# Modulation sums of a two-block model on one core: shared accumulators, fp32r row sums, and filler transposes at two seams

## The reference

```python
def reference(...):                      # 39 arrays, the first is x (1, 256, 2048)
    x = first_block(x, ...)              # attention + gated linear attention, then
                                         # x + (silu(h @ w_gate) * (h @ w_up)) @ w_down
    return second_block(x, c_2, ...)

def second_block(x, c, ...):
    c_act = jax.nn.silu(c)
    mod = (c_act @ w_ada[l] + b_ada[l])[:, None, :]        # w_ada is 2048 x 12288
    sh1, sc1, g1, sh2, sc2, g2 = jnp.split(mod, 6, axis=-1)
    h = rms_norm(x, norm_mix[l]) * (1.0 + sc1) + sh1
    x = x + g1 * hybrid_mixer(h, ...)
    h = rms_norm(x, norm_ffn[l]) * (1.0 + sc2) + sh2
    x = x + g2 * conv_glu_ffn(h, ...)                      # up, conv of width 3, silu gate, down
    return rms_norm(x, norm_final)
```

## Time and profile before

| | us |
|---|---|
| median of 3 runs | 2351.09 |
| range of the runs | 2350.31 to 2352.11 |
| profiled execution, its own time | 2352.51 |
| its span, first to last instruction | 2350.7 |
| PE busy | 2337.8 (99%) |
| DVE busy | 1616.4 (69%) |
| ACT busy | 1153.2 (49%) |
| mean granted TensorE clock | 0.997 of full |
| DMA, mean over the span | 543.62 MB, 231 GB/s |

### The profile page before, as it was taken

How to read it: one execution, slowest core, us unless ns; L and a number is a source line. 1 busy time by engine, 2 the same in 40 slices (tenths; PEclk the granted TensorE clock), 3 DMA queues, 4 the chain that set the end, 5 groups by cost and what they waited for, 6 DMA issues and landing times.

```text
span 2350.7 us, 43754 instructions
## 1 busy us (share of the span) xinstructions
PE 2337.8 (99%) x17937; PEld 2151.6 (92%) x17937; DVE 1616.4 (69%) x1931; ACT 1153.2 (49%) x1510; POOL 5.1 (0%) x7
## 2 busy tenths in 40 slices
PE   9999999999999999999999999999999999999998
PEld 8889778999999999888999899888999999998887
DVE  5668568777777766877778455667878666665556
ACT  5565454534344344444764444546544445454444
POOL 0000000000000000000000000000000000000000
PEclk9999999999999999999999999999999999999999
DMA  8556567888888877898577545555778656665563
GB/s 308 167 179 197 159 234 271 278 282 297 282 282 295 282 242 263 316 324 315 175 279 269 163 130 153 196 200 187 283 255 295 208 179 206 196 206 197 192 192 117
DMA packets 233049, 543.62 MB, mean 231 GB/s; under 512 B 15610, under 2 KB 22596, under 8 KB 232260
## 3 DMA queue, kind: packets, MB, share of 16 engines
q1 hardware_dynamic: 232756, 540.97, 68.3%
q10 hardware_dynamic: 144, 0.52, 0.1%
HBM read 535.11 MB, written 6.32 MB: 230 GB/s over the span
## 4 chain that ended last, share of the span: by engine, by line
PE 98%; DVE 0%; ACT 0%; issue 0%; DMA 0%; SPq 0%; DVEq 0%; ACTq 0%
PE ps L330 37%; PE ps L1858 18%; PE ps L608 18%; PE ps L2216 16%; PE ps L1875 2%; PE ps L2509 0%; PE ps L1041 0%; PE ps L1053 0%; PE ps L1071 0%; PE ps L1083 0%; PE ps L2141 0%; PE ps L460 0%; PE ps L2744 0%; PE ps L1134 0%; PE ps L2921 0%
## 5 line engine op out<-in xcount | busy, mean ns | idle before, releaser
L297 DVE TENSOR_TENSOR weights_lo<-raw_weights,weights_hi 128x1024 fp32r<-128x1024 f32 x786 | 957.6, 1224 | 659.8 <-ACT weights_hi L289 658.0
L289 ACT ACTIVATE weights_hi<-raw_weights 128x1024 fp32r<-128x1024 f32 x782 | 827.2, 1062 | 1086.8 <-PE ps L330 446.4
L516 DVE SCALAR_TENSOR_TENSOR ada_acc<-ada_w,col,ada_acc 128x1024 f32<-128x1024 f32 x180 | 230.2, 1279 | 0.1
L330 PE MATMUL ps<-conv_x_hi,weights_hi 128*128 128x256 f32 x1280 | 198.0, 277 | 0.0
L330 PE MATMUL ps<-glu_x_hi,weights_hi 128*128 128x256 f32 x1280 | 197.7, 276 | 0.0
L330 PE MATMUL ps<-glu_x_hi,weights_lo 128*128 128x256 f32 x1280 | 197.2, 276 | 0.0
L330 PE MATMUL ps<-glu_x_lo,weights_hi 128*128 128x256 f32 x1280 | 197.2, 276 | 0.0
L330 PE MATMUL ps<-conv_x_lo,weights_hi 128*128 128x256 f32 x1280 | 197.2, 276 | 0.0
L330 PE MATMUL ps<-conv_x_hi,weights_lo 128*128 128x256 f32 x1280 | 197.2, 276 | 0.0
L330 PEld LDWEIGHTS ps<-conv_x_hi,weights_hi 128*128 128x128 f32 x1280 | 169.1, 188 | 1.0 <-issue 1.0
L330 PEld LDWEIGHTS ps<-glu_x_hi,weights_hi 128*128 128x128 f32 x1280 | 169.0, 188 | 0.0
(11 more groups left out here) (560 smaller groups left out, 3635.3 us busy)
## 6 DMA issues: line engine op xcount, KB each, us to landing
raw_weights<-in_w_in_dram SPq DMA_DIRECT2D x202, 512.0 KB, 5.0
ada_w<-in_w_ada_dram SPq DMA_DIRECT2D x96, 1024.0 KB, 6.1
raw_weights<-in_w_ffn_up_dram SPq DMA_DIRECT2D x176, 512.0 KB, 4.6
raw_weights<-in_w_gate_dram SPq DMA_DIRECT2D x88, 512.0 KB, 4.6
raw_weights<-in_w_up_dram SPq DMA_DIRECT2D x88, 512.0 KB, 4.6
raw_weights<-in_w_down_dram SPq DMA_DIRECT2D x88, 512.0 KB, 5.7
raw_weights<-in_w_ffn_down_dram SPq DMA_DIRECT2D x88, 512.0 KB, 4.3
raw_weights<-in_w_out_dram SPq DMA_DIRECT2D x64, 512.0 KB, 5.1
```

Source lines behind the costliest of these rows:

```text
L289: kit.nc.scalar.activation(kit.slots(n, i)[0], raw, ACT.Copy).then_inc(kit.w_hi, 1)
L297: kit.nc.vector.tensor_tensor(lo, raw, hi.bitcast(F32), ALU.subtract).then_inc(kit.w_lo, 1)
L330: ins = nc.tensor.matmul(out, lhsT=lhsT, rhs=rhs, start=start and m == 0, stop=(k == KT - 1 and m == 2), skip_group_check=True)
L516: step = nc.vector.scalar_tensor_tensor(acc, w, c, acc, ALU.mult, ALU.add)
```

## The change

**Shared accumulators.** A step no longer takes 128 rows of one group. For groups 0 to 7 a step takes 16 rows of 8192 columns: row `r` and group `g` lie on partition `8 r + g`. One accumulator then holds all eight groups, each on every eighth partition, and 128 steps go over the 2048 rows, numbered as the steps of groups 0 to 7 were. For groups 8 and 9 a step takes 64 rows of 2048 columns, with 32 steps. Groups 10 and 11 stay as they were. The number of steps stays 192. Each step has its own DMA of 0.5 MB (192 DMAs). The accumulator is passed on: `Glu` ends with `ada_acc`, `Down` goes on from it into `ada_acc_oct` and then starts `ada_acc_half`, and the second mixer goes on from that into `ada_acc_9`.

**Columns of c.** The scalars for these steps are `c_2` repeated 8 times (`c_oct`, 128 columns) and twice (`c_half`, 32 columns). They are loaded as rows, widened by two DVE copies, and turned: the eighth pack is 128 wide instead of 96 and there is a ninth. In `Glu` a copy of 16 columns (`c_turn`) is made on DVE once a pass.

**Sums.** Nothing is summed in `Glu`. At seam 1 one set of eight matmuls against the mask `oct` (8 columns) gives all eight groups, at seam 2 one against `half` (2 columns) gives both. DVE adds the bias in `Ada.summed`. `last_scales` goes, and ACT's wait for it.

**Row sums.** Groups 10 and 11: ACT rounds the accumulator (`acc_hi`), DVE computes `acc_lo`, PE makes four fp32r matmuls of 512 columns for a group.

**Fillers.** At seam 1 `keep_busy` puts eight transposes before the turns, at seam 2 eleven in place of eight transposes of an accumulator and three fillers.

**The load of `final_w`** moves from ahead of `Down` to its load of unit pair 12, and waits there for `Down`'s first modulation step.

```diff
     def load(self, sp, lead, j, m):
...
-        w = kit.ins["w_ada_2"][0]
-        sp.dma_start(self.w[:, m % 2, :, :], w[2 * m * P:2 * (m + 1) * P, ds(2 * UN * lead + 2 * UN * j, 2 * UN)]
-                     .rearrange("(k p) n -> p k n", p=P)).then_inc(kit.ada_w[m % 2], 16)
+        for s in (2 * m, 2 * m + 1):
+            sp.dma_start(self.w[:, m % 2, s % 2, :], self.source(lead, j, s)).then_inc(kit.ada_w[m % 2], 16)
+    def source(self, lead, j, s):
+        w = self.kit.ins["w_ada_2"][0]
+        if lead < 8:
+            rows = w[ds(OCT * (16 * lead + s) + 16 * OCT * j, OCT), 0:16 * UN]
+        elif lead < 10:
+            rows = w[HALF * (16 * (lead - 8) + s):HALF * (16 * (lead - 8) + s + 1), 16 * UN:20 * UN]
+        else:
+            rows = w[P * s:P * (s + 1), 2 * UN * lead:2 * UN * (lead + 1)]
+        return rows.rearrange("r (g n) -> r g n", n=2 * UN)
...
+    def sums(self, pe, bank, mask, acc):
+        kit, (a, b) = self.kit, self.kit.at[mask]
+        n = b - a
         for q in range(8):
-            step = nc.tensor.matmul(kit.ps[:, bank, q:q + 1], lhsT=self.acc[:, q * P:(q + 1) * P],
-                                    rhs=kit.c("ones")[:, 0:1], start=True, stop=True)
+            step = kit.nc.tensor.matmul(kit.ps[:, bank, n * q:n * (q + 1)], lhsT=acc[:, q * P:(q + 1) * P],
+                                        rhs=kit.c(mask), start=True, stop=True)
         step.then_inc(kit.ada_sum, 1)
...  Glu, PE and DVE
-            mid = (lambda: self.ada.turned(pe, self.lead, j)) if summed else None
-                if summed and s == begun:
-                    self.ada.reduced(dve, self.lead, j)
-                    self.ada.product(dve, self.lead, j, 8 * half + s // 2)
+                    if q == 0:
+                        nc.vector.tensor_copy(self.c_turn[:, :], kit.col[:, ds(a + 16 * j, 16)]).then_inc(self.s_c, 1)
+                        dve.wait_ge(self.s_c, 1 + j)
+                    self.ada.product(dve, self.lead, j, q, c=self.c_turn[:, q:q + 1])
...  Down, SP
-        sp.wait_ge(kit.ada_sum, self.lead)
-        sp.dma_start(self.final_w[:, :], self.final_src).then_inc(kit.loaded, 16)
+                if k == 12:
+                    sp.wait_ge(kit.ada_acc, 16 * self.lead + 1)
+                    self.load_final(sp)
...  second mixer, PE
-        self.down.ada_sums(pe, 0)
-        self.down.ada_sums(pe, 1, 0, 2)
+        self.down.ada_sums(pe)
         pe.wait_ge(self.squares_in, 11)
         for k in range(4):
             self.turned.turn_early(pe, k)
-        self.down.ada_sums(pe, 1, 2, 8)
+        keep_busy(kit, 8, 7, S)
         for k in range(4):
             self.turned.turn(pe, k)
...  second mixer, DVE
+        self.down.ada_summed(dve)
         modulation(kit, 0)
         dve.wait_ge(self.s_root, 1)
...  ConvGlu
-        pe.wait_ge(kit.ada_acc, 16 * (self.lead + g + 1))
+        pe.wait_ge(self.s_acclo, g + 1)
         for b in range(2):
-            step = nc.tensor.matmul(kit.ps[:, 4 + 2 * g + b, :], lhsT=kit.c("ones"),
-                                    rhs=self.ada.acc[:, b * UN:(b + 1) * UN], start=True, stop=True)
+            for acc in (self.acc_hi, self.acc_lo):
+                step = nc.tensor.matmul(kit.ps[:, 4 + 2 * g + b, :], lhsT=self.ones[:, :], rhs=acc[:, b * UN:(b + 1) * UN],
+                                        start=acc is self.acc_hi, stop=acc is self.acc_lo)
         step.then_inc(kit.ada_sum, 1)
...
-                keep_busy(kit, 3, 7, S)
+                keep_busy(kit, 11, 7, S)
```

More of the change, by code:

```diff
@@ L503, in product, with scalar @@
+    def scalar(self, lead, s):
+        name, first = ("c_oct", 0) if lead < 8 else ("c_half", 8) if lead < 10 else ("c_2", lead)
+        return self.kit.cols(name, 16 * (lead - first) + s)
+    def product(self, dve, lead, j, s, acc=None, prior=None, c=None):
         nc, kit = self.kit.nc, self.kit
         m, k = s // 2, s % 2
[L505 to L509, removed]
@@ L827, in sync @@
         for n in range(1, len(self.packs)):
-            for at, to, width, src in self.packs[n][0]:
-                sp.dma_start(self.pack[at:to, n, 0:width], src).then_inc(self.s_packs, 16)
+            for at, to, lo, hi, src in self.packs[n][0]:
+                tile = {OCT: self.c_rows, HALF: self.c_rows_2}[hi] if hi in (OCT, HALF) else self.pack[:, n, :]
+                sp.dma_start(tile[at:to, lo:hi], src).then_inc(self.s_packs, 16)
         bias = self.mem["bias_dram"].ap()
@@ L944, in turn_pack @@
         _, w, _ = self.packs[n]
-        kit.nc.tensor.transpose(kit.ps[:, 6, 0:w], self.pack[0:w, n, :], kit.c("ident")[0:w, 0:w]
-                                ).then_inc(self.s_packT, 1)
+        last = n == len(self.packs) - 1
+        if n >= len(self.packs) - 2:
+            pe.wait_ge(self.s_cwide, 2)
+        rows = self.pack[0:w, 0 if last else n, :]
+        kit.nc.tensor.transpose(kit.ps[:, 6, 0:w], rows, kit.c("ident")[0:w, 0:w]).then_inc(self.s_packT, 1)
     def spread_scale(self, at):
@@ L1197, in scalar_side @@
             a = COLS["c_2"]
-            kit.act(nc.scalar.activation(kit.col[:, a:a + KT], kit.col[:, a:a + KT], ACT.Silu))
+            nc.scalar.activation(kit.col[:, a:a + KT], kit.col[:, a:a + KT], ACT.Silu).then_inc(self.s_csilu, 1)
+        if n == self.PACK + len(self.packs):
+            act.wait_ge(self.s_col, len(self.packs))
+            for a, b in ((COLS["c_half"], COLS["b_ada_2"]), (COLS["c_oct"], NCOLS)):
+                step = nc.scalar.activation(kit.col[:, a:b], kit.col[:, a:b], ACT.Silu)
+            step.then_inc(self.s_csilu, 1)
         for p in self.parts:
@@ L3574, in __init__ @@
             kit.sem("conv_" + n) for n in ("taps", "base", "sums", "silu", "glu"))
-        self.s_gate, self.s_scales = kit.sem("gate2_bias_in"), kit.sem("last_scales")
+        self.s_gate = kit.sem("gate2_bias_in")
+        self.acc_hi, self.acc_lo = (t(f"ada_acc_{n}", at, [P, 2 * UN], R32) for n, at in (("hi", 60), ("lo", 64)))
+        self.ones = t("ones_rounded", 92, [P, P], R32)
+        self.s_acchi, self.s_acclo = (kit.sem(n) for n in ("ones_and_ada_acc_hi", "ada_acc_lo"))
         self.down = None
@@ L3610, in scale_sums @@
     def scale_sums(self, pe):
-        kit, mixer = self.kit, self.mixer
-        pe.wait_ge(mixer.s_accs, 16)
-        pe.wait_ge(kit.pair_free[0], self.uses[0] + 1)
-        for q in range(8):
-            step = kit.nc.tensor.matmul(kit.ps[:, 1, q:q + 1], lhsT=mixer.accs[:, 0, q * P:(q + 1) * P],
-                                        rhs=kit.c("ones")[:, 0:1], start=True, stop=True)
-        step.then_inc(kit.ada_sum, 1)
-        pe.wait_ge(mixer.s_xlast, ST)
-        turn_sums(kit, mixer.accs[:, 1, :], 2).then_inc(kit.ada_sum, 1)
@@ L3722, in body @@
                         self.turned.scale_first(act, 3 + u // 2)
+                    g = self.acc_split(i, j, u, 1)
+                    if g is not None:
+                        act.wait_ge(kit.ada_acc, 16 * (self.lead + g + 1))
+                        if g == 0:
+                            nc.scalar.activation(self.ones[:, :], kit.c("ones"), ACT.Copy)
+                        else:
+                            act.wait_ge(kit.ada_sum, 2 + g)
+                        nc.scalar.activation(self.acc_hi[:, :], self.ada.acc, ACT.Copy).then_inc(self.s_acchi, 1)
                     if (j, u) == (1, 3):
```

229 lines of the change are left out of this document (100 added, 129 removed).

## The result

The changed kernel took 2421.0 us (median of 4 runs, 2394.4 to 2425.1) against 2351.6 before. The ratio of the means, with a fifth run of 2410.3 in it, is 1.0267, 95% interval 1.0203 to 1.0331. The forecast was 2342.0, faster by 0.4%. It is slower by 2.7%, and its runs lie 31 us apart where those before lay 2 apart. The profiled execution is the fastest of the four, 2394.39 us with a span of 2392.6; what its trace shows is thus 42 us of a loss whose median is 69; two longer executions of the same form of load are taken up further down.

The account below looks back on a forecast made before the run. PE was taken to bound the kernel (busy 2337.8 of 2350.7 us). Terms −5.5 − 1.7 − 2.2 (seam 1) + 0.1 + 0.2 = −9.1 us took the median 2351.09 to 2342.0, 8-in-10 range 2340.0 to 2345.8.

Parts of the forecast that it names:

- Loads: Modulation's 192 DMAs of 0.5 MB for 96 of 1 MB, and final_w among Down's loads: taken to cost 0.
- the loads come late (slower): Rival: the modulation's new load form slows the DMA queues and PE waits, +14 us in Down at 20%, 2356; chance 0.08.
- turned groups in `Glu`: Eight PE transposes for each of groups 0 to 5 go from the Glu passes: −5.5 us.
- row sums: Groups 10 and 11: four fp32r matmuls replace two fp32 ones and the slower products behind them: −1.7 us.
- seam 1, up to the turns: Less one-column work on PE lets the turns start at 1151.45 in place of 1152.32: −0.9 us.
- seam 1, clock: Clock stays full behind seam 1's turns: −1.46, with +0.2 for the next block, together −1.3 us.
- seam 2: DVE's bias step must end before the mean's last step, on the path; PE's queue keeps its length: +0.1 us.
- ninth pack: First mixer: PE turns one more pack, a unit taking 2.91 us against 2.72 without: +0.2 us.
- The DMA setup-cost knee: Skill's rule, about 2 us fixed cost a transfer: 192 us for 96 more DMAs without overlap; the prediction took 0.

Follow-up runs that it names:

- e5: Changed kernel, but loads of groups 0 to 7 take 4 KB from each of 128 rows, named as 16 outer rows of 8: median 2409.6 us.
- e8: Changed kernel, but loads of groups 0 to 7 take 4 KB from each of 128 rows, named as 32 outer rows of 4: median 2343.0 us.
- e9: Changed kernel with each modulation step's load, in all groups, cut into two DMAs of 0.25 MB to 64 partitions each: median 2372.8 us.
- e2: Changed kernel, but the 16 rows of each load of groups 0 to 7 lie 128 rows apart in memory: median 2410.2 us.
- e1: Changed kernel, but loads of groups 0 to 7 take 128 rows of 1024 columns again, one DMA of 0.5 MB a step: median 2343.6 us.
- e3: Changed kernel, but loads of groups 0 to 7 take 32 rows of 4096 columns, each on four partitions: median 2343.3 us.
- e4: Changed kernel, but loads of groups 0 to 7 take 64 rows of 2048 columns, each on two partitions: median 2343.2 us.
- e7: e3 without the eight filler transposes at seam 1: median 2344.5 us, ratio 0.9966 to the kernel before.

## Why the prediction was wrong

**The step that failed** is "Loads": "the bytes and the pieces of 4 KB are the same ... I take 0." The loads cost not 0 but 51 us in the profiled execution, and 67 in a longer one (e5). The pieces are the same; how the DMA names them is not. I had looked at the load as bytes and piece sizes, and the slow thing is the count of outer rows, which the diff shows (`OCT` rows) and no row of the trace before could have priced, since the loads of the modulation and of the weights all had 128 there. One argument of that step failed as well: SP's waits for a slot were read as a sign of room. In the changed kernel SP still waits as much, and PE waits too:

```profile
SPq L258 <- DVE weights_lo L302: 1408.5, 645, 7.4
```

The direction stood among the rivals, "the loads come late (slower)", with the right condition (a share of 1 in the queues), at 8 in 100 and 2356 us.

**How that rival was mis-sized.** Against e8, which differs from the changed kernel in the form of the loads alone, the profiled execution loses 51.4 us of span (2392.6 against 2341.2). The first product of `Down` starts at 939.76 against 902.73 and the sums of seam 1 at 1193.82 against 1142.23, the first rows of each pair being the changed kernel's:

```profile
939.76 0.73 PE L1862 MATMUL ps<-weights_hi,down_hi 128*128 128x512 f32 x2
...
1193.82 1.84 PE L514 MATMUL ps<-cst,ada_acc_oct 128*128 128x8 f32 x16
```

```profile
902.73 0.73 PE L1862 MATMUL ps<-weights_hi,down_hi 128*128 128x512 f32 x2
...
1142.23 1.84 PE L514 MATMUL ps<-cst,ada_acc_oct 128*128 128x8 f32 x16
```

Up to the first product of `Down` 37.0 us are lost, nearly all in `Glu`, and 14.6 in `Down`. Of the 51.4, 34.2 are time in which PE stands (48.2 against 14.0 us of the span) and 17.2 are longer busy time (2344.4 against 2327.2), of which the lower mean clock, 0.996 against 0.999, explains some 7 us as an estimate. For `Down` I had said 14, and that was luck: I took packets 20% longer, and from 960 to 1100 us they take 243 ns on average against e8's 181, 34% longer.

For `Glu` I had said that 17% of room protects it. From 520 to 860 us of e8, 7738 packets of 4 KB with a mean of 181 ns and 32264 of 2 KB with a mean of 98.8 fill 0.84 of the 16 engines' time. In the changed kernel the means are 268 and 106.5. As an estimate, e8's packets at these times would fill 1.01, so that the stream falls below what PE eats; DVE then waits for `ada_w`, `weights_lo` comes late, and PE stands. The measured share is 0.94, with fewer packets (7272 and 29631). At e9's means, 251 and 98.4 ns, the share is 0.96 and PE doesn't wait, and in the changed kernel itself PE is busy 99.85 of 100 us from 320 to 420 at a share of 1.01. So the share says where trouble is near, and not by itself that PE waits.

**The longer executions.** Other traces of the same form, near the median, show what the fast one doesn't. In e5 (2410.2 us) the first product of `Down` lies 36.0 us behind e8's (2 of them from before `Glu`) and the sums of seam 1 67.3, so `Down` lost 31 in place of 14.6, and PE's clock fell there:

```profile
960.00:1100.00 140.00, 122.78 (x496) 99.36 (x495) 85.00 (x87) 49.57 (x61) 0.10 (x1) 0.91 1.01 256
```

e2 (2411.1 us) shows the same, 34 and 68 us.

**The other terms** can be read in e8 and in the changed kernel, and were right:

| term | forecast | measured | where |
|---|---|---|---|
| turned groups in `Glu` | −5.5 | −5.6 | the hi products start 467.9 to 906.8 before and 467.3 to 901.5 in e8: −4.7 for five groups, and −0.6 at the start, in spite of the +0.3 of the ninth pack, for the first |
| row sums | −1.7 | −1.6 | 1775.24 to 1778.50 for sum and 20 products, 4.05 before |
| seam 1, up to the turns | −0.9 | −0.9 | 3.83 in e8 from sums to turns, 4.73 before |
| seam 1, clock | −1.3 | −1.3 | 4.23 and 3.48 for the two blocks, 5.80 and 3.18 before; the forecast's own numbers, −1.46 and +0.22, give −1.2 |
| seam 2 | +0.1 | +0.1 | 1655.32 to 1659.12 in the changed kernel, 3.66 before |
| ninth pack | +0.2 | +0.2 | 66.42 for the first L1026, 66.18 before |

Rows of the changed kernel at the row sum and at seam 2:

```profile
1775.24 0.40 PE L3616 MATMUL ps<-ada_acc_hi,ones_rounded 128*128 128x512 f32 x1
...
1776.17 0.64 PE L335 MATMUL ps<-conv_x_hi,weights_hi 128*128 128x256 f32 x4
...
1778.50 0.62 PE L335 MATMUL ps<-conv_x_hi,weights_lo 128*128 128x256 f32 x4
```

```profile
1655.32 0.60 PE L2145 MATMUL ps<-cst,conv_scaled 128*128 128x128 f32 x4
...
1659.12 0.68 PE L2134 MATMUL ps<-cst,conv_scaled 128*128 128x128 f32 x4 [0.27 <-DVE conv_scaled L2123]
```

The sum was −9.1; the span of e8 lies 9.5 below that of before and its median 8.7 below. The rule of the Trainium skill, "SBUF — State Buffer", The DMA setup-cost knee, weighed beside that step, had no part: with 96 DMAs more, e1, e3, e4 and e8 lie within 1.2 us of the forecast gain (8.0 to 8.7 us below the kernel before, against 9.1). What stays open is why the packets are slow, that is whether engines meet at a port, and why one execution of this form loses twice as much in `Down` as another.

## What to carry to other kernels

When a load changes its access pattern, compare the outermost dimension, not only bytes, piece size and partitions: 16 outer rows made the median packet of 4 KB 70% slower than 32, 64 or 128 outer rows, and loads to 64 partitions did the same with 64 outer rows. Price such a load in share of the DMA engines' time, for every stage that runs beside it, and take a share near 1 as a warning: here a stage at 0.82 was lost as surely as one at 0.88, and one at 0.96 (e9, `Glu`) was not. And a load that only an off-path product needs is on the path as soon as that product stands in an in-order list ahead of work that isn't.

## What I had not expected of the hardware

- The same 0.5 MB from the same DRAM addresses to the same 128 partitions lands in 7.9 us (median over the kernel) named as 16 x 8 pieces and in 5.3 named as 32 x 4 (e5, e8).
- The same DMA queues move 365 GB/s beside 64-row loads and 265 to 277 beside 16-row loads in one kernel.
- The loads of the second gate, 128 rows in one DMA or 64 rows to 64 partitions in each of two, have packets of 159 and of 278 ns at the median (changed kernel, e9).
- Eight transposes of the identity in a gap of 1.5 us kept TensorE at 2.4 GHz (granted clock 1.00); without them it ran at 1.2 GHz (0.50) for the six us behind the gap (e3, e7).
- All kernels with slow packets scatter: the runs of the changed kernel lie 31 us apart and those of e2 12, those of e8 0.5. Why, no run here shows.
